# A single-core hybrid decoder layer: another prologue and another place for the first convolution

## The reference

```
h    = rms_norm(x, norm_w)
proj = h @ w_in                      # 2048 x (4*4*128 + 4*6*128 + 12 + 4*6*128)
retention       (4 heads)  on rq, rk, rv, gate rg
gated DeltaNet  (6 heads)  on silu(causal_conv(gqkv)), gate gz,
                beta = sigmoid(gb), g = -exp(a_log) * softplus(ga + dt_bias)
block attention (6 heads)  on mq, mk, mv, gate mz
out  = x + concat(y_ret, y_gdn, y_moba) @ w_out
```

## Time and profile before

| what | us |
|---|---|
| median of 3 runs | 529.79 |
| lowest and highest of them | 528.07 and 530.11 |
| the profiled execution, device time | 528.16 |
| its span in the trace | 526.3 |
| PE busy | 515.7 |
| DVE busy | 331.0 |
| ACT busy | 275.9 |

### The profile page before, as it was taken

How to read it: one execution, slowest core, us unless ns; L and a number is a source line. 1 busy time by engine, 2 the same in 40 slices (tenths; PEclk the granted TensorE clock), 3 DMA queues, 4 the chain that set the end, 5 groups by cost and what they waited for, 6 DMA issues and landing times.

```text
span 526.3 us, 8792 instructions
## 1 busy us (share of the span) xinstructions
PE 515.7 (98%) x3493; PEld 435.8 (83%) x3493; DVE 331.0 (63%) x523; ACT 275.9 (52%) x437; POOL 76.1 (14%) x70
## 2 busy tenths in 40 slices
PE   6999899999999999999999999999999999999997
PEld 6878788888888888888888888888888888888885
DVE  2868999898866777655644464655456445556451
ACT  4667645564346566655545554564465465433440
POOL 0036243333312213210000000100010001000000
PEclk9999999999999999999999999999999999999999
DMA  8996657556745464666666667667765557657711
GB/s 270 322 289 153 174 145 185 138 157 161 202 123 127 117 159 121 162 162 182 169 177 188 161 162 199 159 159 196 204 170 164 167 181 220 192 189 217 263 40 40
DMA packets 147130, 91.67 MB, mean 174 GB/s; under 512 B 7987, under 2 KB 136082, under 8 KB 147090
## 3 DMA queue, kind: packets, MB, share of 16 engines
q1 hardware_dynamic: 143456, 88.81, 61.5%
q10 hardware_dynamic: 3634, 2.31, 1.5%
HBM read 89.00 MB, written 2.10 MB: 173 GB/s over the span
## 4 chain that ended last, share of the span: by engine, by line
PE 92%; DVE 6%; DMA 1%; ACT 0%; issue 0%; ACTq 0%; DVEq 0%
PE pj L1408 19%; PE pj L1407 19%; PE pj L1405 19%; PE pj L1383 10%; PE pj L1384 5%; PE pj L1453 3%; DVE w_lo L337 2%; DVE big L935 2%; PE pj L1462 1%; PE mx L1549 1%; PE mx L1439 1%; PE mx L1599 1%; PE mx L1582 1%; PE mx L1497 1%; PE mx L1668 1%; PE mx L1432 1%
## 5 line engine op out<-in xcount | busy, mean ns | idle before, releaser
L337 DVE TENSOR_TENSOR w_lo<-w_raw,w_hi 128x1024 fp32r<-128x1024 f32 x160 | 196.9, 1237 | 93.3 <-ACT w_hi L431 92.5
L431 ACT ACTIVATE w_hi<-w_raw 128x1024 fp32r<-128x1024 f32 x159 | 167.8, 1058 | 140.2 <-PE pj L1408 113.7
L1405 PE MATMUL pj<-w_hi,hT 128*128 128x512 f32 x320 | 127.5, 398 | 0.0
L1407 PE MATMUL pj<-w_hi,hT 128*128 128x512 f32 x320 | 126.0, 394 | 0.0
L1408 PE MATMUL pj<-w_lo,hT 128*128 128x512 f32 x320 | 125.0, 391 | 0.0
L1383 PE MATMUL pj<-hT,w_hi 128*128 128x512 f32 x300 | 108.8, 402 | 1.3 <-DVE w_lo L337 1.3
L1384 PE MATMUL pj<-hT,w_lo 128*128 128x256 f32 x300 | 84.0, 280 | 0.0
L1408 PEld LDWEIGHTS pj<-w_lo,hT 128*128 128x128 f32 x320 | 60.1, 188 | 12.4
L1405 PEld LDWEIGHTS pj<-w_hi,hT 128*128 128x128 f32 x320 | 60.2, 188 | 11.7
L1407 PEld LDWEIGHTS pj<-w_hi,hT 128*128 128x128 f32 x320 | 60.3, 188 | 11.3
L1383 PEld LDWEIGHTS pj<-hT,w_hi 128*128 128x128 f32 x300 | 56.4, 188 | 14.1 <-DVE w_lo L337 2.0
(11 more groups left out here) (231 smaller groups left out, 487.1 us busy)
## 6 DMA issues: line engine op xcount, KB each, us to landing
w_raw<-in_w_in_dram SPq DMA_DIRECT2D x256, 256.0 KB, 3.4
w_raw<-in_w_out_dram SPq DMA_DIRECT2D x64, 256.0 KB, 3.9
big<-in_x_dram SPq DMA_DIRECT2D x14, 256.0 KB, 6.0
out_dram<-sq ACTq DMA_DIRECT2D x7, 256.0 KB, 5.9
cst<-table_dram SPq DMA_DIRECT2D x1, 554.0 KB, 8.8
big<-in_x_dram SPq DMA_DIRECT2D x4, 128.0 KB, 3.3
cst<-table_dram ACTq DMA_DIRECT2D x1, 132.0 KB, 3.8
out_dram<-sq ACTq DMA_DIRECT2D x1, 128.0 KB, 2.5
```

What stands on the lines that cost most here:

```text
L337: eng.tensor_tensor(w_lo[:, n % NSPLIT, :], w_raw[:, n % NRAW, :], w_hi[:, n % NSPLIT, :].bitcast(F32), ALU.subtract).then_inc(S("lo"), 1)
L431: act.activation(w_hi[:, n % NSPLIT, :], w_raw[:, n % NRAW, :], ACT.Copy).then_inc(S("hi_done"), 1)
L1405: ins = pe.matmul(bank[:, :], src[:, kc, 0, tok], hi[:, k, :], start=first, stop=False)
L1407: pe.matmul(bank[:, :], src[:, kc, 1, tok], hi[:, k, :], start=False, stop=False)
```

## The change

PE starts with 11 products of zeros (`er[:, 0, :]`, which POOL clears first) and no longer waits for the identity before its first instruction; after block 0 of x come 4 such products in place of 16 transposes. Each piece of x is one DMA, so SP issues five where it issued ten. Of the constant table only the identity is loaded early; the rest comes in one DMA on SP's queue after tile 7. The two k of block 0 go to two PSUM banks, and ACT alternates: hT of k=0, first half of w_hi of tile 0, hT of k=1, second half. In the gate chain `conv(0, 0, 0)` and the w_lo of tile 11 go ahead of z; the w_lo of tiles 12, 14 and 15 move ahead of a step of the chain or of a convolution; `decay_sums` goes ahead of `conv(1, 0, 0)`.

```
+        def first_bank(k):
+            return mx[2] if k == 1 else mx[k // 2 % 4]
...
-            for c in range(C):
-                eng.dma_start(x_sb[:, c, piece], x[0, c * P:(c + 1) * P, piece]).then_inc(S(f"x_in{i}"), 16)
+            eng.dma_start(x_sb[:, :, piece], x[0, :, piece].rearrange("(c p) n -> p c n", p=P)).then_inc(S(f"x_in{i}"), 16)
...
-                    sp.dma_start(cst[:, K_FIRST:], table[:, K_FIRST:]).then_inc(S("cst_in2"), 16)
+                    sp.dma_start(cst[:, P:], table[:, P:]).then_inc(S("cst_in"), 16)
...
-            act.wait_ge(S("pad_zero"), 1)
+            act.wait_ge(S("pad_zero"), 2)
             act.activation(sm[:, 44:45], raw[:, 0, 0, 0:1], ACT.Copy)
-            act.dma_start(cst[:, P:K_FIRST], table[:, P:K_FIRST]).then_inc(S("cst_in"), 16)
...
-            def first_high_part():
-                for k, done, made in ((0, "w_first", "hi_first"), (1, "w_in0", "hi_done")):
-                    act.wait_ge(S(done), 16)
-                    act.activation(w_hi[:, 0, k * 512:(k + 1) * 512], w_raw[:, 0, k * 512:(k + 1) * 512], ACT.Copy).then_inc(S(made), 1)
+            def first_high_part(k):
+                done, made = (("w_first", "hi_first"), ("w_in0", "hi_done"))[k]
+                act.wait_ge(S(done), 16)
+                act.activation(w_hi[:, 0, k * 512:(k + 1) * 512], w_raw[:, 0, k * 512:(k + 1) * 512], ACT.Copy).then_inc(S(made), 1)
...
                 for k in range(2 * b, 2 * b + 2):
-                    act.activation(hT[:, k, 0, :], mx[b % 4][:, k % 2 * T:(k % 2 + 1) * T], ACT.Copy,
+                    act.activation(hT[:, k, 0, :], first_bank(k)[:, k % 2 * T:(k % 2 + 1) * T], ACT.Copy,
                                    scale=pcol[:, R_NORM + k:R_NORM + k + 1]).then_inc(S("h_hi"), 1)
+                    if b == 0:
+                        first_high_part(k)
                 if b == 0:
-                    first_high_part()
                     high_part(1)
...
+            pool.memset(er[:, 0, :], 0.0).then_inc(S("pad_zero"), 1)
             pool.memset(raw[:, :, :, 0:PAD], 0.0).then_inc(S("pad_zero"), 1)
...
-                dve.wait_ge(S("h_hi"), 2 * b + 2)
                 for k in range(2 * b, 2 * b + 2):
+                    dve.wait_ge(S("h_hi"), k + 1 if b == 0 else 2 * b + 2)
...
+            conv(0, 0, 0)
+            advance(70)
             dve.wait_ge(S("bias_in"), 2 * 16)
             dve.wait_ge(S("tanh_b"), 1)
...
             dve.tensor_tensor(ab[:, A_T1], ab[:, A_Z], ab[:, A_T1], ALU.min).then_inc(S("negabs_z"), 1)
-            conv(0, 0, 0)
-            advance(74)
+            advance(77)
             conv(0, 1, 0)
...
             conv(0, 0, 1)
-            advance(92)
+            advance(93)
             conv(0, 1, 1)
-            advance(100)
+            advance(101)
             dve.wait_ge(S("ln_u"), 1)
...
             advance(112)
+            decay_sums()
+            advance(117)
             conv(1, 0, 0)
-            advance(118)
-            decay_sums()
+            advance(119)
             conv(1, 1, 0)
...
                 for _ in range(n):
-                    pe.transpose(mx[2][:, 0:P], ident, ident)
+                    pe.matmul(pj[3][:, 0:HALF], er[:, 0, :], er[:, 0, 0:HALF], start=True, stop=True)
...
+            pe.wait_ge(S("pad_zero"), 1)
+            keep_busy(11)
             pe.wait_ge(S("ident_in"), 2 * 16)
             pe.transpose(mx[3][:, 0:KC], prow[0:KC, :], ident[0:KC, 0:KC]).then_inc(S("norm_psum"), 1)
-            keep_busy(3)
...
             all_x_blocks(0)
-            keep_busy(16)
+            keep_busy(4)
```

More of the change, by code:

```diff
@@ L638, in solve @@
                 act.wait_ge(S("gm"), LEVELS - 2)
-                act.wait_ge(S("pad_zero"), 3)
+                act.wait_ge(S("pad_zero"), 4)
                 for a in (0, QUART):
@@ L893, in _ @@
             for b in range(KC // 2):
-                dve.wait_ge(S("h_hi"), 2 * b + 2)
                 for k in range(2 * b, 2 * b + 2):
-                    dve.scalar_tensor_tensor(hT[:, k, 1, :], mx[b % 4][:, k % 2 * T:(k % 2 + 1) * T], pcol[:, R_NORM + k:R_NORM + k + 1],
+                    dve.wait_ge(S("h_hi"), k + 1 if b == 0 else 2 * b + 2)
+                    dve.scalar_tensor_tensor(hT[:, k, 1, :], first_bank(k)[:, k % 2 * T:(k % 2 + 1) * T], pcol[:, R_NORM + k:R_NORM + k + 1],
                                              hT[:, k, 0, :].bitcast(F32), ALU.mult, ALU.subtract).then_inc(S("h_lo"), 1)
@@ L939, in _ @@
             dve.wait_ge(S("cst_in"), 16)
-            dve.wait_ge(S("cst_in2"), 16)
             steps = [0]
@@ L1431, in x_blocks @@
                 for k in range(2 * b, 2 * b + 2):
-                    ins = pe.transpose(mx[b % 4][:, k % 2 * T + c * P:k % 2 * T + (c + 1) * P],
+                    ins = pe.transpose(first_bank(k)[:, k % 2 * T + c * P:k % 2 * T + (c + 1) * P],
                                        x_sb[:, c, k * P:(k + 1) * P], ident)
@@ L1466, in first_group_low @@
                     ins.then_inc(S("tile_used"), 1)
+            pe.wait_ge(S("pad_zero"), 1)
+            keep_busy(11)
             pe.wait_ge(S("ident_in"), 2 * 16)
             pe.transpose(mx[3][:, 0:KC], prow[0:KC, :], ident[0:KC, 0:KC]).then_inc(S("norm_psum"), 1)
-            keep_busy(3)
             def all_x_blocks(b):
-                pe.wait_ge(S(f"x_in{b if b < 2 else b // 2 + 1}"), 16 * C)
+                pe.wait_ge(S(f"x_in{b if b < 2 else b // 2 + 1}"), 16)
                 if b == 3:
@@ L1514, in _ @@
             pe.wait_ge(S("cst_in"), 16)
-            pe.wait_ge(S("cst_in2"), 16)
             for c in range(C):
```

## The result

The changed kernel is slightly slower: ratio to the kernel before 1.0034, 95% interval 1.0025 to 1.0043, medians 530.62 and 528.65 us over 16 executions each. That is 1.8 us more, where 3.7 us less was forecast. The profiled execution has a span of 529.6 us against 526.3: this pair of executions is 3.3 us apart, more than the medians are. One execution of the kernel before, on the chip of e1 to e4, took 1327.64 us and is left out of every figure.

A forecast was written before the change was run, and what follows sets the result against it. PE, busy 515.7 of 526.3 us, was taken as the bound. Prologue 1.45 us plus gate chain 2.25 us make 3.7 us off the 529.0 mean, so 525.3 us, range 523.3 to 528.4.

The forecast's parts named there:

- the supply step: Prologue: tile 2 lands 0.7 us earlier, its products start near 15.15; wrong if they start before 14 or after 16.
- the clock step: Prologue: PE is at its high clock for x's transposes; wrong if those of block 1 take 0.85 us.
- the chain step: Gate chain: gains 2.25 us with a 0.35 us wait at unit 116; wrong if PE's hole at L1525 exceeds 1 us.
- What PE waits for: Gate chain: PE's waits of 1.2 and 1.4 us go, and the rest of the run moves up as it is.
- Price of the zero products: Prologue: each 128x64 zero product costs 0.21 to 0.40 us; 11 take 2.4 to 4.4, taken as 2.4 to 2.9.
- norm_w at 3.9: Prologue: identity and norm_w land at 3.9 us, after the first zero products are over, so these cost nothing.
- The 1.9 us of spare time ahead of tile 2: Prologue: from 6.2 PE needs 7.0 us before tile 2, could be there at 13.2, so 1.9 us are spare.
- The clock in the prologue: Prologue: PE runs at the high clock from the first needed product at 6.2; a low clock until about 9.8 costs nothing.
- the change doesn't do what it says with the clock: Prologue rival, chance 0.10: clock stays low, until 14.5 if holes keep it so; tile 2's products at 17.35; 527.5 us.
- Tile 2 as the limit: Prologue: tile 2's landing caps the gain at 1.45 us, bounds 0.7 and 3.1, with its products at 15.15.
- The rival that I worked out by it: Gate chain: by the skill's port rule two taps cost 1.46 us, not 0.8; unit 116's wait is 1.0, not 0.35.
- a fall of the clock behind the holes of the prologue: Slower rival, chance 0.06: clock falls behind holes before tiles 1 and 2, costing 3.24 us per first-group tile; 531.8 with two.

The follow-up runs named there:

- e1: The changed prologue with the DVE order (gate chain) of the kernel before; ratio to the kernel before 1.0021 (1.0010 to 1.0031).
- e4: As e1, with 3 zero products of 256 columns in place of 11 of 64, and 1 in place of 4 after block 0; ratio 0.9983.
- e2: The changed gate chain with the prologue of the kernel before; ratio to the kernel before 1.0025 (1.0008 to 1.0042).
- e5: As e1, with 6 zero products of 64 columns in place of 11 before the identity's wait; ratio to the kernel before 1.0002.
- e12: The changed kernel with advance(101) back to advance(100), so tile 15's w_lo is behind g; ratio to the kernel before 0.9980.
- e8: The changed kernel with e4's wide zero products, and conv(0, 1, 1) and tile 15's w_lo behind g; ratio to the kernel before 0.9952.
- e9: As e2, with 18 unread transposes on PE just ahead of its wait for g at unit 116; ratio to the kernel before 0.9976.

## Why the prediction was wrong

Both terms of the sum failed. The prologue was to give 1.45 us and alone costs 1.1 (e1); the gate chain was to give 2.25 us and alone costs 1.3 (e2). By the signs that the forecast named for itself, the supply step failed (tile 2 at 18.07, after 16), the clock step in the main (block 1's transposes took 0.74 us, between 0.44 and 0.85), and the chain step (a hole of 2.2 us at the running sums, more than 1).

**What PE waits for: right.** Both old waits in the chain went, and the late part of the run moved with the early one, but for the 0.4 us at L1604.

**Price of the zero products: the far bound, passed.** I put 0.21 to 0.40 us on one and took the near end, by the columns; it was 0.45. The float32 product has a floor that doubles with the clock, which the earlier trace rows offered as the other end (0.40). They ran until 5.94, later than the 5.3 that was to cost nothing.

**norm_w at 3.9: wrong.** The forecast kept this landing of before. Behind a merged piece of x it comes at about 4.7, so block 0 could not be transposed before that with any number of products.

**The 1.9 us of spare time ahead of tile 2: too large, and spent twice.** PE's work from the first product to tile 2 was put at 7.0 us; before it takes 7.34, because PE waits 0.14 us for hT of block 1 and the eight products of tile 1 take 2.09 and not 1.84. That leaves 1.6 us. By the sum above a start 1.4 us late would still have brought PE to tile 2 at 14.9 at the high clock, and a low clock until 9.8 behind a start at 6.2 at 15.3, next to the 15.15 set by the weights. Each was covered or nearly so; the forecast never put them together. e5 has both, a start at 7.65 and a rise at 9.8: 16.04.

**The clock in the prologue: wrong, and in the rival's direction.** The sum took the high clock from the first product on, and against the rival I carried "the rise came 5.3 us after the first instruction" over from one execution. Rises seen with the old prologue were 9.2, 9.8, 9.0, 6.8 and 9.0, with the new one 12.8, 9.7 and 10.2: one trace gave neither the place nor its spread. The rival "the change doesn't do what it says with the clock" (0.10) was the nearest for this stage, with tile 2 at 18.07 in the profiled execution against its 17.35; but in the executions of e1 and e12 with the earlier rise it was 16.64 and 16.87.

**Tile 2 as the limit: right mechanism, not reached.** It holds in e8 to within 0.4 us, in an execution with an early rise. In the changed kernel nothing waits for tile 2.

**g: mis-sized by 1.7 us.** In times of before g was forecast at 58.97; measured 62.15 less the 1.48 us of later start, 60.7. The wait at unit 116 was to be 0.35 and was 2.2. The work was as counted; what was mis-sized is the term for POOL, 0.8 for the moved taps less 0.56 given back by the chain's own step. Against it the rows show: the moved convolution +0.46 (2.77 in place of 1.51 + 0.8); the two w_lo behind it and behind z +0.53 and +0.55; the step given back is met again (L962, 0.76 in place of 0.17), +0.59; the last steps of g +0.54 (two meetings in place of the one of before); and conv(0, 1, 0), which no longer meets POOL, -0.86. Together that is +1.8.

The Trainium skill's rule ("SBUF — State Buffer", section "Who interferes with whom") names the w_lo among those hit, since w_lo too has two SBUF inputs. The price that the page's section "Summary: rules for kernel authors" gives, the second to start blocked until the first is done, is not what the rows show, 0.4 to 0.6 us per meeting with a POOL operation of 0.72 to 0.91. And two of the steps that were hit, L962 and L987, have one input, so the rule on two inputs does not speak of them. The rival that I worked out by it put the wait at 1.0, nearer than mine and still 1.2 us short, because it too counted the taps alone.

**A fall of the clock behind the hole: put at nothing in the sum.** I gave 0.06 to a fall of the clock behind the holes of the prologue, and took the 1.38 us hole at 66.95 as proof that holes do no harm. The mechanism was right and the place wrong. Joining two holes of 1.2 and 1.4 us into one of 2.2 us makes the sum smaller and the clock fall, 1.7 us for each stretch; filling the hole gave e9 2.6 us over e2, and removing it gave e12 2.9 us over the changed kernel. With the later start of the prologue this is why a kernel with less waiting was slower.

## What to carry to other kernels

Where PE is the bound, count holes one by one and not their sum: here those of 1.2 and 1.4 us cost their length, and one of 2.2 us cost in most executions 1.7 us more in the clock behind it. When a dependent chain is moved on a crowded engine, price every instruction that comes to lie beside GpSimd, not the moved one alone. When loads are merged, ask which small load stands behind them. Before a filler goes ahead of the critical path, take the dear end of its price, since it delays what stands behind it. A clock that rises at a time of its own needs several executions before a sum may rest on it.

## What the runs showed of the hardware

- A float32 product of 128x64 costs 0.45 us at the low clock, one of 128x256 0.98 us (6 records in 2.93 us, e8 and e4): a quarter of the columns for nearly half of the time.
- The granted clock reads 1.00 from the start of every trace until the first rise and is only true after it; the length of the products shows the low level there.
- Behind a hole of 2.2 us the granted clock fell to 0.50 for 3.4 us in one profiled execution (the changed kernel) and not in another (e2); the mean clocks say that it fell at least once in nine of e2's 12 executions and in all 16 of the changed kernel, and in none of e9's 11 with the hole filled. Behind holes of 1.2 and 1.4 us it did not fall in any of 34.
- Products of zeros, 128x256, lifted the clock in e8 at 4.31 us, when PE had done nothing else; behind the same six records in e4 it rose at 10.2. Behind the 128x64 ones no trace has a rise before 9.7.
- A vector step of 12 elements takes 0.17 us alone and 0.58 to 0.76 beside a GpSimd operation; a w_lo 1.22 and 1.75 to 1.77.
- An 8 KB load on ScalarE's queue (norm_w) landed 3.3 to 3.8 us after its issue when x's pieces were one DMA each, and 2.5 to 3.2 when they were two (14 traces).
